# A hybrid encoder layer in split FP32: four rearrangements of transfers and clears around the scan

## The reference

```python
u = x @ w_in                                  # 1024 x 7688
oa = gdn(ua); ob = rwkv7(ub); oc = swa(uc)     # gated DeltaNet | RWKV-7 | windowed attention
merged = g0 * (oa @ w_a) + g1 * (ob @ w_b) + g2 * (oc @ w_c)
x = layer_norm(ALPHA * x + merged @ w_out)
x = layer_norm(ALPHA * x + (silu(x @ gate) * (x @ up)) @ down)
```

## Time and profile before

| | |
|---|---|
| median of 3 runs | 1791.92 us (1790.76 to 1796.33) |
| profiled execution | 1793.21 us, of which 1791.4 us from first to last instruction |
| mean granted TensorE clock | 0.996 of full speed |
| busy: PE, DVE, ACT, POOL | 1759.7, 1210.3, 712.5, 530.7 us |
| instructions | 28296 |
| moved by DMA | 293.25 MB, mean 164 GB/s |

### The profile page before, as it was taken

One profiled execution on the slowest core, in us unless ns is written; L12 is line 12 of the kernel. 1 busy time (PEld: TensorE's weight loads), 2 busy tenths in 40 slices (PEclk: granted clock), 3 DMA queues, 4 the chain that ended last, 5 costly groups with the idle time before them and its releaser, 6 DMA issues. The chain is left out here.

```text
span 1791.4 us, 28296 instructions
## 1 busy us (share of the span) xinstructions
PE 1759.7 (98%) x11040; PEld 1450.3 (81%) x11040; DVE 1210.3 (68%) x1503; ACT 712.5 (40%) x1218; POOL 530.7 (30%) x404
## 2 busy tenths in 40 slices
PE   9999999999999999899999999999999999999997
PEld 8778888777788887788877888888888888888886
DVE  3856675768579974677768745956666656655578
ACT  3534444234454434455632221343333333344241
POOL 1211221222211002244324642854555545400000
PEclk9999999999999999999999999999999999999999
DMA  6256675135673365878375553245454454479464
GB/s 181 50 110 140 148 173 150 49 93 156 170 190 108 116 174 157 240 252 255 114 264 175 177 195 94 83 131 164 135 165 153 162 184 148 165 271 316 161 223 156
DMA packets 369925, 293.25 MB, mean 164 GB/s; under 512 B 155916, under 2 KB 301900, under 8 KB 367744
## 3 DMA queue, kind: packets, MB, share of 16 engines
q1 hardware_dynamic: 293568, 237.63, 44.5%
q10 hardware_dynamic: 76224, 53.81, 10.4%
HBM read 196.33 MB, written 94.98 MB: 163 GB/s over the span
## 5 line engine op out<-in xcount | busy, mean ns | idle before, releaser
L170 PE MATMUL bank<-xhi,w_hi 128*128 128x512 f32 x608 | 241.7, 398 | 1.4 <-DVE xlo L1216 0.7
L172 PE MATMUL bank<-xhi,w_lo 128*128 128x512 f32 x608 | 237.4, 390 | 0.0
L171 PE MATMUL bank<-xlo,w_hi 128*128 128x512 f32 x608 | 236.8, 389 | 0.0
L547 POOL TENSOR_TENSOR w_lo<-w_raw,w_hi 128x1024 fp32r<-128x1024 f32 x37 | 103.1, 2788 | 359.4 <-ACT w_hi L973 359.4
L2409 POOL TENSOR_TENSOR ff_ring_lo<-ff_w_sums,ff_ring_hi 128x512 fp32r<-128x512 f32 x88 | 124.4, 1415 | 76.7 <-ACT ff_ring_hi L2691 76.7
L2409 POOL TENSOR_TENSOR ff_ring_lo<-ff_raw,ff_ring_hi 128x512 fp32r<-128x512 f32 x66 | 95.8, 1452 | 149.1 <-ACT ff_ring_hi L2691 149.1
L170 PEld LDWEIGHTS bank<-xhi,w_hi 128*128 128x128 f32 x608 | 114.2, 188 | 28.4 <-issue 5.7
L172 PEld LDWEIGHTS bank<-xhi,w_lo 128*128 128x128 f32 x608 | 114.1, 188 | 24.8
L171 PEld LDWEIGHTS bank<-xlo,w_hi 128*128 128x128 f32 x608 | 114.3, 188 | 22.5
L177 PE MATMUL b_ps<-x1hi,ff_ring_hi 128*128 128x512 f32 x264 | 102.9, 390 | 0.0
L179 PE MATMUL b_ps<-x1hi,ff_ring_lo 128*128 128x512 f32 x264 | 102.7, 389 | 0.0
(11 more groups left out here) (502 smaller groups left out, 4690.5 us busy)
## 6 DMA issues: line engine op xcount, KB each, us to landing
w_raw<-in_w_in ACTq DMA_DIRECT2D x49, 512.0 KB, 4.3
hid_ops<-y SPq DMA_DIRECT2D x77, 256.0 KB, 2.8
ff_raw<-hid_ops SPq DMA_DIRECT2D x77, 256.0 KB, 3.8
op<-opnd SPq DMA_DIRECT2D x16, 1152.0 KB, 5.6
b_gate<-u SPq DMA_DIRECT2D x24, 512.0 KB, 3.5
u<-work ACTq DMA_DIRECT2D x44, 256.0 KB, 3.6
ff_raw<-in_ffn_gate SPq DMA_DIRECT2D x22, 512.0 KB, 4.1
ff_raw<-in_ffn_up SPq DMA_DIRECT2D x22, 512.0 KB, 5.6
```

What stands on the lines that cost most here:

```text
L170: pe.matmul(out, w_hi, x_hi, start=first, stop=False)
L171: pe.matmul(out, w_hi, x_lo, start=False, stop=False)
L172: return pe.matmul(out, w_lo, x_hi, start=False, stop=last)
L547: pool.tensor_tensor(w_lo[b][:, :, :], w_raw[b][:, :, :], as_f32(w_hi[b][:, :, :]), ALU.subtract).then_inc(w_lo_done, 1)
```

## The change

It has four parts. **Inverse stores:** the two X stores also wait for `mm_p` to reach `AT[4, 7] + 2`. **Scan loads:** for chunks 2 and up the three inverse DMAs are issued ahead of the seven operand DMAs. **Start of the scan:** the clears of `sv[0]` move to the end of phase 1 (DVE), those of `attn` to POOL behind the first `decay_state`; the last sum goes behind the first strict masks on DVE, its sigmoid and store behind the first `rwkv_residuals` on ACT; the load of the ALiBi table moves from SP's queue to the head of ACT's; and for chunk 0 DVE's order is join, causal, gdn masks, softmax instead of causal, join, softmax, gdn masks. **Branch weights:** `load_w(q + 3)` is issued in step q, where `load_w(q + 2)` was, from step 1 on.

```diff
 def load_chunk(sp, c, tiles, opnd, xinv, landed, inv_landed):
+    load_inverse(sp, c, tiles, xinv, inv_landed)
     load_operands(sp, c, tiles, opnd, landed)
-    load_inverse(sp, c, tiles, xinv, inv_landed)
...
                     if which == 0:
                         sp.wait_ge(inv_step[0], CORNERS_END[0] + R)
+                        sp.wait_ge(mm_p, AT[4, 7] + 2)
...
-            for tile in early[1]:
-                for e in range(2):
+            for e in range(2):
+                for tile in early[1]:
                     step(dve.memset(tile[rwkv_rows(1 - e), 4 * e:4 * e + 4, 1, :], 0.0))
+                step(dve.memset(early[2][0][rwkv_rows(e), 4 * e:4 * e + 4, :], 0.0))
...
-                if i == 0:
-                    sp.dma_start(alibi[:, :], const_dram[:, ALIBI_COL:]).then_inc(alibi_landed, 16)
...
-            last_sum(dve)
-            for e in range(2):
-                dve.memset(sv[0][rwkv_rows(e), of(e), :], 0.0).then_inc(s_rw_done, 1)
+            dve.sem_inc(s_rw_done, 2)
             dve.memset(s_g[0][:, :, :], 0.0).then_inc(s_g_done, 2)
-            for b in range(2):
-                dve.memset(attn[b][:, :, :, :], 0.0).then_inc(cleared, 1)
-            dve.wait_ge(cleared, 2)
...
             def gdn_masks(c):
                 dve.wait_ge(mm_a, c + 1)
+                if c == 0:
+                    dve.wait_ge(cleared, 2)
...
             strict_masks(0)
+            last_sum(dve)
             for c in range(NCH):
                 gdn_residuals(c)
-                causal_masks(c)
-                join_inverse(c)
-                softmax_top(c)
-                gdn_masks(c)
+                if c == 0:
+                    join_inverse(c)
+                    causal_masks(c)
+                    gdn_masks(c)
+                    softmax_top(c)
+                else:
...
...
-            last_half()
+            act.dma_start(alibi[:, :], const_dram[:, ALIBI_COL:]).then_inc(alibi_landed, 16)
             inverse_rows(0)
             for c in range(NCH):
                 rwkv_residuals(c)
+                if c == 0:
+                    last_half()
...
                 decay_state(c)
+                if c == 0:
+                    for b in range(2):
+                        pool.memset(attn[b][:, :, :, :], 0.0).then_inc(cleared, 1)
...
             for q in range(NW):
-                if q >= 2 and q + 2 < NW:
-                    load_w(q + 2)
+                if 4 <= q + 3 < NW:
+                    load_w(q + 3)
```

## The result

The changed kernel takes 1796.84 us (median of 20 runs, 1793.96 to 1804.77), the one before 1793.37 in the 20 runs beside them: a ratio of 1.0024 (95% interval 1.0013 to 1.0035), 3.5 to 4.3 us slower. The forecast was 6.3 faster. The profiled execution took 1795.06 (span 1793.2), that of before 1793.21 (span 1791.4): 1.85 of the difference is in this pair of traces.

The account below looks back on a forecast made before the run. PE, busy 1759.7 of 1791.4 us, was taken as the bound. Removing 4.0 + 3.1 + 1.0 = 8.1 and giving back 1.8 nets -6.3, forecasting 1785.6 us against the median, range 1782.7 to 1790.5.

Parts of the forecast that it names:

- The waits 'issue' of 1.2 and 0.7 in chunk 2: Scan, chunk 2: PE waits without a releaser, taken as unchanged; bounds -1.9 to +1.9 us.
- In later chunks POOL does not wait for the inverse: Scan after chunk 2: loading the inverse first changes nothing, as buffers are three deep; 0 us.
- Pair 10's landing of 7.1: Phase 1: pair 10's second load lands 7.1 us after issue (bounds 4.6 and 9.6), 1.8 given back in all.
- rival 4: Phase 1: pair 10's second load takes 13.9 us, 10.6 given back against 8.1 won, 1794.4 us; chance 0.05.
- rival 3: Phase 1: stall moves to pair 10, PE waits 2.0, clock falls, 4.0 given back, 1787.8 us; chance 0.21.
- Pair 9, 4.0 won: Phase 1: with X stores later, pair 9's loads land uncrowded; the 2.0 wait and the clock come back, 4.0 us.
- Chunk 1 earlier by 1.8: Start of the scan: reordered masks, softmax and clears let PE's second chunk start about 1.8 us earlier.
- the inverse of chunk 2 by 1.3: Scan, chunk 2: with the inverse issued first, PE's wait of 1.3 us at line 1691 goes.
- The clears, last sum and sigmoid: Start of the scan: moving these to idle engine time or behind first masks and residuals costs nothing.
- Weight 23, 1.0 won: Branch weights: weight 23 loads 3 to 4 us earlier, so PE's wait of 1.0 us goes.
- Rival 2: Scan keeps its waits because chunk 2's operands are late or issue waits grow; 3.1 lost, 1788.7 us; chance 0.10.

Follow-up runs that it names:

- e2: Kernel before with only the three inverse loads issued ahead of the seven operand loads for chunks 2 and up; ratio 1.0022.
- e14: Kernel before, its order of loads kept, with the loads from chunk 3 on also waiting for the next chunk's block products (1.6 us later); ratio 1.0042.
- e8: e2 with the large operand load moving only the first half of its columns from chunk 3 on; ratio 0.9969.
- e5: The whole change, but with the inverse loaded ahead of the operands for chunk 2 only; ratio 0.9982.
- e1: Kernel before with only the two X stores also waiting for product (7,8); ratio 1.0004.
- e11: e5 with SP's loads of chunks 0 and 1 held until pair 10's weights have landed; ratio 0.9983.
- e4: Kernel before with only the earlier branch weight loads (weight q+3 issued in step q); ratio 0.9991.
- e13: e5 with SP's loads of chunks 0 and 1 held until snap (6,9) has been made; ratio 0.9947.
- e7: Kernel before with the loads from chunk 3 on also waiting for the next chunk's residual products (3.3 us later); ratio 1.0000.
- e9: e2 with the same added wait as e7, its loads 3.3 us later; ratio 1.0009.
- e10: e2 with the large operand load split into two halves, each followed by three of the six small loads; ratio 0.9984.

## Why the prediction was wrong, point by point

1. *"The waits 'issue' of 1.2 and 0.7 in chunk 2 have no releaser; ... I take no change."* This is the step that failed: issue waits were taken as fixed, and the reordered loads of chunks 3 and up as free. They are PE's instruction fetches held back by large loads, and the change moved those loads in every chunk from 2 on. The bounds of 1.9 either way were sized on chunk 2 alone; there both did go (the 5.5 at chunk 3), but behind it 6.0 appeared, and 9.3 with restarts and clock. e2 alone reproduces the loss, e14 without the swap too, e8 and e5 remove it.
2. *"In later chunks POOL does not wait for the inverse ...: nothing."* I looked at who waits for the inverse and for the operands, not at what the large load passes on its way. The order that was worth about 3.4 us in chunk 2 was a loss in the others.
3. *Pair 10's landing of 7.1, between bounds of 4.6 and 9.6.* The second load took 12.6 from its issue at 680.0 and landed at 692.6. From the 680.6 of the prediction that is 12.0, past the upper bound and past the 11.4 from which rival 4 decides; by rival 4's sum 8.7 would have been given back. It was 3.65: PE stood 3.3 and the clock did not fall, so phase 1 gained 0.35 where I had 2.2. That is rival 3, the stall moves, with a chance of 0.21. Its price of 4.0 is nearly met, though not by its terms (2.0 for the snap and as much for the clock), and e1 agrees within its interval. Two things were mis-sized. The bounds came from rows that had met one competitor, and 4.6 was the middle of two loads (3.9 and 5.3) where 9.6 was a second load alone. And a late snap was charged to PE in full, while the prediction's own row shows a slack of some 2 us: in the kernel before the snap at 676.42 was 4.1 behind the end of its product and PE stood 2.0; here it was 5.6 behind and PE stood 3.3, most of it for the low part of pair 10's weights, a wait that the prediction does not name. Nor was the clock's fall to be counted on either way: it did not come behind this wait of 2.8, and it did behind e11's 3.1 (0.88 in 700 to 712).
4. *Pair 9, 4.0 won*: right in place (high part at 666.71, products at full clock), and given back by point 3.
5. *Chunk 1 earlier by 1.8, the inverse of chunk 2 by 1.3.* Right: 1.9 (1.5 from the block's begin, since phase 1 gave 0.35) and 3.15 at chunk 2. The clears, last sum and sigmoid cost nothing, as forecast.
6. *Weight 23, 1.0 won*: right, its wait is gone; e4's -0.09% agrees but its interval holds zero.
7. *Rival 2* named grown issue waits, in chunk 2, at a price of 3.1 with a chance of 0.10. They grew, but in the chunks behind it, and cost 9.3, three times the price.

Parts that came out: -0.35, -5.2 to chunk 3, -2.0 in phase 3; and +9.3, hence +1.8 between the two spans. In the prediction's sums the ends of the range are 0.1 off their own terms (1782.6 and 1790.6), which changes nothing.

## What to carry to other kernels

A wait of TensorE without a releaser in a stretch full of transfers can be a transfer too: look for the instruction queue's packets in the DMA view, and treat every edit that moves a large load as one that can move them, most of all a steady-state order changed for the sake of one iteration. A burst of transfers that is put off will meet whatever the other queue sends next; follow it until it lies behind everything that is waited for (e11 stopped one store short of that, e13 did not). Before a bound for a landing is taken from a row, count what ran beside that row, and see which of several loads it is.

## What the runs showed that was not expected

- The instruction fetch costs by where the load lies, and not monotonically. SP's issue of the large load behind the end of the chunk's outputs, and the issue waits from chunk 3 on: 0.04 us (before, most chunks), 0.3 us of waits; 1.6 to 2.6 (e14), 5.5; 1.4 to 3.3 (after and e2), 6.0 and 9.6; 3.4 to 4.6 (e7), 2.2; 4.7 or more (e9), 0.8. That a fetch asked for at about 2 us gets through ahead of a load that starts behind 3 fits most of them; the request itself isn't in the trace. Nor is the hold strict: e9 has an instruction packet in 842.5 to 843.0, with a large load issued at 839.78 that took 6.1 to landing.
- By the Trainium skill (DMA: Bandwidth & Descriptors, "Queues, rings and completion order") DMA engines take turns between queues packet by packet, a packet being 9 to 17 descriptors as a rule and 64 at most. The large load has 128 rows of 9216 B, as an estimate 8 for each of 16 engines, so by the Trainium skill an engine's part may be a single packet, and a fetch or a store that stands back for the whole of it agrees with that. No run here shows where such a packet ends, so this stays an explanation that was not tested; that two halves with small loads between them hold PE less (e10) fits it.
- The second of two loads of 512 KB took 5.3 us to landing with little beside it, 9.6 beside X stores and 12.6 beside SP's loads (1.9 MB for chunk 0); a store of 256 KB took 7.7 beside the same loads in e11.
- Splitting one load of 1152 KB into two with small ones between costs SP one more issue per chunk, and saved 0.38% against the same order unsplit (e10 against e2; the two come from different comparisons).
